# Three float32r layers on one core: starting addresses inside the SBUF arena shifted by 64 and 192 bytes

## The chip, the core and the metric

The kernel runs on one core of one Trainium2 chip. The metric is the device time of one execution in microseconds (us); here the median of three executions.

## What is computed

The reference puts three layers behind each other for one sequence of 512 tokens with 1,024 features, in float32. Cut to what matters:

```python
def first_block(x, ...):                        # DEPTH = 2
    for i in range(DEPTH):
        mix = ssd_mixer(x, ...) if i % 2 == 0 else hgrn2_mixer(x, ...)
        h = layer_norm(ALPHA * x + mix, ...)
        a = relu(h @ w1[i])                     # 1024 -> 4096
        h = layer_norm(ALPHA * h + (a * a) @ w2[i], ...)
        x = h + sigmoid(h @ w_gate[i]) * (p[i] @ w_proj[i])
    return x

def second_block(x, mem, positions, ...):       # DEPTH_2 = 1
    x = mla_layer(x, mem, ...)                  # 12 heads of 96, 4 memory heads of 64
    return rmsnorm(x, final_norm_g)
```

`ssd_mixer` is a state space layer in chunks of 128 tokens, `hgrn2_mixer` a gated linear recurrence with 8 heads. Nearly all of the arithmetic lies in the products with weights: the projections into and out of each mixer, the two MLPs, the gates.

## The kernel before

It is written by hand, engine by engine, with semaphores. Each engine has its own program in a block; the order on TensorE (PE) is fixed in the text.

**Split products.** A float32 product is made of three float32r products. Each operand is split into a high part (a float32r copy) and a low part (what the copy lost, rounded to float32r). For each 128-row slice k of the inner dimension, TensorE then multiplies high by high, high (stationary) by low (moving), low (stationary) by high (moving). `times_parts` (L889, the multiplication at L907) does so for the out-projections, both MLPs, the gates and most of the third layer; `passes` (L699, at L702) for the first layer's projections, the attention scores, the small projections of the third layer and the last product; an inner `passes` of `hgrn_project` (L1078, at L1081) for the HGRN heads, where the moving operand is 512 columns wide for two of the units and 256 for the other two; `gate_tile` (L988, at L1001) for the first tile of a gate. In a profile's name such as `psum<-w_lo,hid_hi` the moving operand stands first and the stationary one second. The stationary operand is 128 columns, and is loaded by a LDWEIGHTS of its own for every multiplication (PEld).

```python
for n_pass, (a, m_) in enumerate(((still_hi, moving_hi), (still_hi, moving_lo), (still_lo, moving_hi))):
    m = pe.matmul(psum[:, bank[c], cols or slice(0, width)], a, m_, start=..., stop=...)
```

**Where operands come from.** Weights come by DMA in units of 1,024 x 512 floats into two slots in turn (SP's queue). ScalarE (ACT) copies each unit to `w_hi` (L1654), VectorE (DVE) subtracts to `w_lo` (L2432), both slice by slice, behind TensorE's use of the previous unit. Activations are turned on TensorE, and their parts written by ACT (`f_hi`, `hid_hi`) and DVE (`f_lo`, `hid_lo`).

**The memory.** All buffers have fixed addresses in a partition of SBUF. `slots`, `res`, `rn`, `fT`, `gb` and `pT` are tensors of their own, each a multiple of 4,096 bytes long. After them lies the arena (L158) of 29,920 floats, which the stages share: `carve` (L169) hands out float32 views one after the other, `part` (L223) puts a float32r tensor at a given word of it, `over` (L226) one over the other tensors. The main ones, by word of the arena:

```python
yT_lo = [part("yT_lo_a", 13824, KD, T), part("yT_lo_b", 9728, KD, T)]
rings = [part(f"ring{n}", ring_first + n * KD * 256, KD, 256) for n in range(3)]   # ring_first = 17920
f_hi, f_lo = part("f_hi", 5632, KD, T), part("f_lo", 13824, KD, T)
w_hi, w_lo = part("w_hi", 17920, KD, HALF), part("w_lo", 22016, KD, HALF)
hid_hi, hid_lo = part("hid_hi", 0, KD, T), part("hid_lo", 9728, KD, T)
```

The arena begins at byte 103,328, which is 160 beyond a multiple of 256. So does every one of the tensors above, and so do the slots and `fT`: at L907 the moving operand and every stationary tile start at the same place within 256 bytes. A stationary tile is 512 bytes of a partition, a moving operand of 512 columns 2,048.

Of the kernel before, what the change touches and what calls it, by code (L numbers as in the profile page):

```python
# [12 lines left out]
F32R = mybir.dt.float32r  # L13
# [3 lines left out]
P = 128  # L17
T = 512
NT = T // P
D = 1024  # L20
KD = D // P
# [5 lines left out]
RMS_EPS = 1e-5  # L27
EPS = 1e-6
ARENA = 29920
DFF = 4 * D  # L30
KF = DFF // P
PLE = 256
# [18 lines left out]
NMEM = 256  # L51
MT = NMEM // P
# [45 lines left out]
    return c  # L98

class Banks:

# [28 lines left out]
def build(nc, x, p, cst, par_a, par_b, w_ssd, w_dt, dt_bias, a_log, d_skip, w_ssd_out, w_hgrn, w_hgrn_out,  # L132
          ln_g, ln_b, w_mlp1, w_mlp2, w_gate, w_proj, mem, pos, w_mla, w_uq, w_ukv, w_mem, w_mla_out, fin_g, out):
    with ExitStack() as ctx:
        def sb(name, shape, dt=F32):
            return ctx.enter_context(nc.sbuf_tensor(name, shape, dt))
# [18 lines left out]
        gb_base = nc.sbuf_base - 4 * 2 * D  # L155
        pT = sb("pT", [P, DEPTH, KP, T])
        pT_base = nc.sbuf_base - 4 * DEPTH * KP * T
        arena = sb("arena", [P, ARENA])  # L158
        arena_base = nc.sbuf_base - 4 * ARENA
        con = sb("con", [P, C_ALL])  # L160
        col_b = sb("col_b", [P, B_ROWS])
        eps_h = sb("eps_h", [P, 1])
# [4 lines left out]
        at = [0]  # L167

        def carve(*shape):  # L169
            n = int(np.prod(shape))  # L170
            assert at[0] + n <= ARENA, (at[0], n)
            v = arena[:, at[0]:at[0] + n]
            at[0] += n
            if len(shape) == 2:
                v = v.rearrange("p (a b) -> p a b", a=shape[0])
            if len(shape) == 3:
                v = v.rearrange("p (a b c) -> p a b c", a=shape[0], b=shape[1])
            return v

        xdt = carve(NT, HALF)
        xw = carve(NT, HALF)
        xr = carve(NT, HALF)
        zs = carve(NT, HALF)
        prev = carve(NT - 1, HALF)
# [27 lines left out]
        xdt_first, xw_first = 0, 2048  # L213
        dtT = zs[:, 0, :]
        s_par = prev[:, 0, 0:2 * P].rearrange("p (a n) -> p a n", a=2)
        s_p = [arena[:, 26112 + i * NT * PLE:26112 + (i + 1) * NT * PLE].rearrange("p (t n) -> p t n", t=NT)
               for i in range(DEPTH)]
        Mh = rn[:].rearrange("p t d -> p (t d)").rearrange("p (j l) -> p j l", j=S_HPG)
        bc_w = gb[:].rearrange("p a b -> p (a b)").rearrange("p (k n) -> p k n", k=KD)
# [1 line left out]

        def part(name, first, *shape):  # L223
            return nc.alloc_sbuf_tensor_at(name, [P, *shape], F32R, offset=arena_base + 4 * first)

        def over(name, base, *shape):  # L226
            return nc.alloc_sbuf_tensor_at(name, [P, *shape], F32R, offset=base)
# [2 lines left out]
        bc_lo = over("bc_lo", gb_base, KD, 256)  # L230
        x_lo, z_lo = over("x_lo", slots_base, KD, HALF), over("z_lo", slots_base + 4 * 4096, KD, HALF)
        rings = [part(f"ring{n}", ring_first + n * KD * 256, KD, 256) for n in range(3)]
        z_his = [part(f"z_hi{n}", ring_first + n * KD * 256, KD, HALF) for n in range(2)]
        yT_hi = [over("yT_hi_a", fT_base, KD, T), part("yT_hi_b", 0, KD, T)]
        yT_lo = [part("yT_lo_a", 13824, KD, T), part("yT_lo_b", 9728, KD, T)]
        sums_parts, picks = over("sums_parts", pT_base, T), over("picks", pT_base + 4 * T, S_HEADS)
# [14 lines left out]
        w_hi, w_lo = part("w_hi", 17920, KD, HALF), part("w_lo", 22016, KD, HALF)  # L251
        hid_hi, hid_lo = part("hid_hi", 0, KD, T), part("hid_lo", 9728, KD, T)

        sq = arena[:, 4096:4096 + 3 * T].rearrange("p (a l) -> p a l", a=3)
        sg = arena[:, 9728:9728 + 4096].rearrange("p (t d) -> p t d", t=NT)

        def pp(i, t):

            return pT[:, i, :, :].rearrange("p k l -> p (k l)") if t == NT - 1 else arena[:, 26112 + t * D:26112 + (t + 1) * D]

        first_hi, first_lo = over("first_hi", fT_base, KD, HALF), z_lo

# [60 lines left out]
        ukv_hi, ukv_lo = part("ukv_hi", 17920, KKV, A_HEADS * 2 * NOPE), part("ukv_lo", 22016, KKV, A_HEADS * 2 * NOPE)  # L323
        out_his = [part("out_hi0", 22016, KD, HALF), part("out_hi1", 16384, KD, HALF)]
        branch_lo = part("branch_lo", 0, KD, T)
        mem_tok = arena[:, 0:MT * D].rearrange("p (a b) -> p a b", a=MT)
        memT = arena[:, MT * D:MT * D + KD * NMEM].rearrange("p (a b) -> p a b", a=KD)
        gate = rn

# [1115 lines left out]
        def _(act):  # L1446
# [235 lines left out]
            def projected(stage, i, j):  # L1682

                t, h = j // NHALF, j % NHALF
                b = full(stage, (h, t))
                act.copy(pp(i, t)[:, h * HALF:(h + 1) * HALF], psum[:, b, :]).then_inc(bank_free[b], 1)
# [470 lines left out]
        def _(dve):  # L2157
# [405 lines left out]
            def half_gate(i, h, t):  # L2563

                cols = slice(h * HALF, (h + 1) * HALF)
                wait_taken(dve, f"gate{i}", (h, t))
                dve.wait_ge(res_ready, NT * (2 * i + 1) + t + 1)
                dve.tensor_tensor(sg[:, t, cols], sg[:, t, cols], pp(i, t)[:, cols], ALU.mult)
                dve.drain()
                dve.tensor_tensor(res[:, t, cols], res[:, t, cols], sg[:, t, cols], ALU.add)\  # L2570
                    .then_inc(sig(f"{('ple_first', 'ple_second')[h]}{i}"), 1)
# [585 lines left out]
```

## Time and profile before

| | |
|---|---|
| median of three executions | 1888.76 us (1887.98 to 1889.18) |
| the profiled execution | 1887.8 us, its span 1885.9 us |
| TensorE, multiplications | 1860.2 us (99%), 9,678 of them |
| TensorE, loads of the stationary operand | 1572.5 us (83%) |
| VectorE | 1139.6 us (60%) |
| ScalarE | 922.0 us (49%) |
| GpSimd | 178.1 us (9%) |
| granted TensorE clock | 0.998 of full speed |
| DMA | 162.02 MB, 86 GB/s over the span |

The time of the profiled execution is what the device reports; the span runs from its first to its last instruction, 1.9 us less. Busy time of PE counts each multiplication from its start to its modelled end; consecutive ones overlap, so the distance from one start to the next (the pace) says more than the 389 ns that one is listed with.

### The profile page before, as it was taken

The page shows a single profiled execution, that of the slowest core. Times are in us where ns is not written, and L with a number is a line of the kernel's source. Part 1 is how long each engine was busy: PE and PEld are TensorE (multiplying, and loading weights), DVE is VectorE, ACT ScalarE, POOL GpSimd, SP SyncE. Part 2 cuts the span into 40 slices and gives each one's busy share as a digit, 9 for nine tenths or more (in the row PEclk, how much of TensorE's full clock was granted, in tenths as well). Part 3 has the DMA queues.
Part 4 walks back from the last instruction along what each step waited for, and adds up shares of the span by engine and source line. Part 5 has one row for each costly group of instructions (what it writes and reads, how often), then busy time and mean ns, then how long its engine had stood idle before and what let it go on. Part 6 is the DMA issues. An engine that isn't in the chain of part 4 may idle for free.

```text
span 1885.9 us, 26981 instructions
## 1 busy us (share of the span) xinstructions
PE 1860.2 (99%) x9678; PEld 1572.5 (83%) x9678; DVE 1139.6 (60%) x2013; ACT 922.0 (49%) x1827; POOL 178.1 (9%) x137
## 2 busy tenths in 40 slices
PE   8999999999999999999999999999999999999998
PEld 7788787877888888899999977888888889887987
DVE  5677677557443434557887876634444587556765
ACT  5765765453332324546768655323333364535551
POOL 0201202004000000400101003100000220001100
PEclk9999999999999999999999999999999999999999
DMA  6131214314233222313312124323222222320001
GB/s 200 45 108 41 76 45 157 112 68 156 89 108 115 90 89 90 89 46 90 91 45 67 46 81 143 112 90 115 106 89 89 90 101 93 117 101 1 1 0 45
DMA packets 116738, 162.02 MB, mean 86 GB/s; under 512 B 6085, under 2 KB 57251, under 8 KB 116643
## 3 DMA queue, kind: packets, MB, share of 16 engines
q1 hardware_dynamic: 115347, 156.04, 24.8%
q0 software_dynamic: 1296, 4.72, 0.7%
q8 instruction: 59, 0.97, 0.2%
q14 instruction: 36, 0.29, 0.0%
HBM read 158.64 MB, written 2.10 MB: 85 GB/s over the span
## 4 chain that ended last, share of the span: by engine, by line
PE 92%; DVE 4%; ACT 3%; DVEq 1%; issue 0%; ACTq 0%; DMA 0%; SPq 0%
PE psum L907 52%; PE psum L702 15%; PE psum L1081 8%; PE psum L667 4%; PE psum L1114 3%; PE psum L1344 2%; PE psum L853 1%; PE psum L940 1%; DVE arena L2275 1%; DVE z_lo L2199 1%; PE psum L1001 1%; PE psum L860 1%; PE psum L848 1%; ACT rn L1548 1%; ACT arena L1542 0%; PE psum L1188 0%
## 5 line engine op out<-in xcount | busy, mean ns | idle before, releaser
L2432 DVE TENSOR_TENSOR w_lo<-slot,w_hi 128x512 fp32r<-128x512 f32 x304 | 232.9, 785 | 352.7 <-ACT w_hi L1654 352.6
L1654 ACT CAST w_hi<-slot 128x512 fp32r<-128x512 f32 x304 | 185.4, 623 | 426.0 <-PE psum L907 410.5
L907 PE MATMUL psum<-f_lo,w_hi 128*128 128x512 f32 x528 | 205.4, 389 | 0.0
L907 PE MATMUL psum<-f_hi,w_hi 128*128 128x512 f32 x512 | 199.8, 390 | 1.4 <-DVE f_lo L2480 1.0
L907 PE MATMUL psum<-w_hi,hid_hi 128*128 128x512 f32 x512 | 199.5, 390 | 0.0
L907 PE MATMUL psum<-w_hi,hid_lo 128*128 128x512 f32 x512 | 199.2, 389 | 0.0
L907 PE MATMUL psum<-w_lo,hid_hi 128*128 128x512 f32 x512 | 199.2, 389 | 0.0
L907 PE MATMUL psum<-f_hi,w_lo 128*128 128x512 f32 x512 | 199.2, 389 | 0.0
L3056 POOL TENSOR_TENSOR res<-rn,gb 128x1024 f32<-128x1024 f32 x16 | 46.2, 2888 | 838.5 <-DVE rn L2420 632.5
L907 PEld LDWEIGHTS psum<-f_lo,w_hi 128*128 128x128 f32 x528 | 99.1, 188 | 20.5 <-issue 0.2
L907 PEld LDWEIGHTS psum<-f_hi,w_hi 128*128 128x128 f32 x512 | 96.1, 188 | 22.9 <-DVE f_lo L2480 1.8
L907 PEld LDWEIGHTS psum<-w_hi,hid_lo 128*128 128x128 f32 x512 | 96.1, 188 | 20.1
L907 PEld LDWEIGHTS psum<-f_hi,w_lo 128*128 128x128 f32 x512 | 96.1, 188 | 20.1
L907 PEld LDWEIGHTS psum<-w_hi,hid_hi 128*128 128x128 f32 x512 | 96.1, 188 | 19.8
L907 PEld LDWEIGHTS psum<-w_lo,hid_hi 128*128 128x128 f32 x512 | 96.1, 188 | 19.7
L907 PE MATMUL psum<-w_hi,f_lo 128*128 128x512 f32 (+2 forms) x224 | 82.5, 368 | 0.0
L702 PE MATMUL psum<-in_hi,ring 128*128 128x512 f32 x192 | 77.0, 401 | 0.0
L702 PE MATMUL psum<-in_lo,ring 128*128 128x512 f32 x192 | 74.8, 389 | 0.0
L667 PE MATMUL psum<-con,arena 128*128 128x128 f32 (+1 forms) x486 | 70.4, 273 | 0.7 <-DVE branch_lo L2977 0.3
L2275 DVE SCALAR_TENSOR_TENSOR arena<-psum,col_a,arena 128x511 f32<-128x511 f32 (+2 forms) x72 | 53.4, 747 | 27.6 <-ACT arena L1536 24.0
L1081 PE MATMUL psum<-w_hi,f_hi 128*128 128x256 f32 x224 | 65.6, 293 | 0.0
L667 PEld LDWEIGHTS psum<-con,arena 128*128 128x128 f32 (+1 forms) x486 | 57.7, 146 | 7.5 <-issue 2.1
(388 smaller groups left out, 4376.1 us busy)
## 6 DMA issues: line engine op xcount, KB each, us to landing
slot<-in_w_mlp SPq DMA_DIRECT2D x128, 512.0 KB, 5.7
slot<-in_w_ssd SPq DMA_DIRECT2D x32, 512.0 KB, 5.8
slot<-in_w_hgrn SPq DMA_DIRECT2D x32, 512.0 KB, 6.7
slot<-in_w_ssd_out SPq DMA_DIRECT2D x16, 512.0 KB, 6.0
slot<-in_w_gate SPq DMA_DIRECT2D x16, 512.0 KB, 5.4
gb<-in_w_ssd SPq DMA_DIRECT2D x8, 512.0 KB, 7.9
slot<-in_w_hgrn_out SPq DMA_DIRECT2D x8, 512.0 KB, 5.8
slot<-in_w_mla SPq DMA_DIRECT2D x8, 512.0 KB, 5.3
```

Source lines behind the costliest of these rows:

```text
L667: return pe.transpose(psum[0:mp, b, cols:cols + kp], src, con[0:kp, C_ID:C_ID + kp])
L702: m = pe.matmul(out, a, m_, start=first and n_pass == 0, stop=last and n_pass == 2)
L848: pe.matmul(psum[:, b, :], Btok[:, c, :], xw[:, c, :], start=True, stop=True).then_inc(bank_full[b], 1)
L853: m = pe.matmul(psum[:, b, j * S_P:(j + 1) * S_P], Mh[:, j, c * P:(c + 1) * P], xdt[:, c, j * S_P:(j + 1) * S_P], start=True, stop=True)
L907: m = pe.matmul(psum[:, bank[c], cols or slice(0, width)], a, m_, start=opens and k == 0 and n_pass == 0, stop=closes and k == KD - 1 and ...
L1081: m = pe.matmul(out, a, m_, start=k == 0 and n_pass == 0, stop=k == KD - 1 and n_pass == 2)
L1114: m = pe.matmul(psum[:, b, c * P:(c + 1) * P], a, a, start=True, stop=True)
L1344: m = pe.matmul(psum[:, b, (t - 1) * V_HEAD:t * V_HEAD], probT[:, (t - 1) % 2, c * P:(c + 1) * P], values(c), **first_and_last(c, nk))
L1654: act.copy(w_hi[:, k, :], as_k(slot_of(stage, n))[:, k, :]).then_inc(high_made, 1)
L2275: m = dve.scalar_tensor_tensor(cv[:, n % 3, back:T], psum[:, b, 0:T - back], col_a[:, at_:at_ + 1], cv[:, n % 3, back:T], ALU.mult, ALU.add)
L2432: dve.tensor_tensor(w_lo[:, k, :], as_k(slot_of(stage, n))[:, k, :], w_hi[:, k, :].bitcast(F32), ALU.subtract).then_inc(low_made, 1)
L3056: pool.tensor_tensor(res[:, t, :], rn[:, t, :], gb[:, 0, :], ALU.mult).then_inc(sig("res_scaled"), 1)
```

## The change

```diff
+GUARDS = ((5632, 0), (9728, 16), (13824, 16), (17920, 16), (22016, 48), (26112, 48))
+ARENA_WORDS = ARENA + GUARDS[-1][1]
...
+def placed(word):
+    return word + max([guard for first, guard in GUARDS if first <= word], default=0)
...
-        arena = sb("arena", [P, ARENA])
-        arena_base = nc.sbuf_base - 4 * ARENA
+        arena = sb("arena", [P, ARENA_WORDS])
+        arena_base = nc.sbuf_base - 4 * ARENA_WORDS
...
-            v = arena[:, at[0]:at[0] + n]
+            v = arena[:, placed(at[0]):placed(at[0]) + n]
...
         def part(name, first, *shape):
-            return nc.alloc_sbuf_tensor_at(name, [P, *shape], F32R, offset=arena_base + 4 * first)
+            at_, n = placed(first), int(np.prod(shape))
+            whole = nc.alloc_sbuf_tensor_at(name, [P, at_ % 8 + n], F32R, offset=arena_base + 4 * (at_ - at_ % 8))
+            v = whole[:, at_ % 8:at_ % 8 + n]
+            return v.rearrange("p (a b) -> p a b", a=shape[0]) if len(shape) == 2 else v
...
-        sq = arena[:, 4096:4096 + 3 * T].rearrange("p (a l) -> p a l", a=3)
-        sg = arena[:, 9728:9728 + 4096].rearrange("p (t d) -> p t d", t=NT)
+        sq = arena[:, placed(4096):placed(4096) + 3 * T].rearrange("p (a l) -> p a l", a=3)
+        sg = arena[:, placed(9728):placed(9728) + 4096].rearrange("p (t d) -> p t d", t=NT)
```

Starts within 256 bytes, counted from the old common one:

| buffers | before | changed |
|---|---|---|
| `hid_hi`, `f_hi`, `yT_hi_b`, `o_hi`, `branch_lo`; outside the arena `in_hi`, `in_lo`, `x_lo`, `z_lo`, `bc_lo`, `m_hi`, `yT_hi_a`, slots | 0 | 0 |
| `hid_lo`, `f_lo`, `yT_lo`, `o_lo` | 0 | 64 |
| `w_hi`, `ring0`, `ring1`, `z_hi`, `qT_hi`, `kT_hi`, `kT_lo`, `out_hi1`, `ukv_hi` | 0 | 64 |
| `w_lo`, `ring2`, `out_hi0`, `ukv_lo` | 0 | 192 |
| `con` (the identity that transposes are made with) | 128 | 64 |

## Rows read from the trace of the kernel before

**Rows 1.** the page, part 1, busy time of each engine, and TensorE's clock in part 2.
```profile
PE 1860.2 (99%) x9678; PEld 1572.5 (83%) x9678; DVE 1139.6 (60%) x2013; ACT 922.0 (49%) x1827; POOL 178.1 (9%) x137
...
PEclk9999999999999999999999999999999999999999
```

**Rows 2.** waits of PE: who ended them, us in total, times, longest.
```profile
PE psum L667 <- DMA rn<-in_x: 5.0, 1, 5.0
PE psum L780 <- ACT rn L1548: 3.6, 4, 1.1
```

**Rows 3.** stretches: all of L907, then L1081, L1001 and L702, on PE and PEld.
```profile
0.00:1886.00 1886.00, 985.32 (x4368) 811.72 (x4368) 1.00 0.26 86
0.00:1886.00 1886.00, 165.52 (x1008) 144.85 (x1008) 1.00 0.26 86
0.00:1886.00 1886.00, 22.61 (x96) 17.88 (x96) 1.00 0.26 86
0.00:1886.00 1886.00, 383.60 (x1692) 297.66 (x1692) 1.00 0.26 86
```

**Rows 4.** timeline of PE in the first MLP: first and last of 28 rows.
```profile
589.24 0.39 PE L907 MATMUL psum<-w_hi,hid_hi 128*128 128x512 f32 x1
...
595.36 0.39 PE L907 MATMUL psum<-w_hi,hid_hi 128*128 128x512 f32 x1
```

**Rows 5.** timeline of PE: 13 rows of L1081, then 18 of L907 at 288 columns.
```profile
879.74 0.28 PE L1081 MATMUL psum<-w_lo,f_hi 128*128 128x256 f32 x1
...
881.18 0.28 PE L1081 MATMUL psum<-w_lo,f_hi 128*128 128x256 f32 x1
1592.87 0.29 PE L907 MATMUL psum<-w_hi,m_hi 128*128 128x288 f32 x1
...
1593.40 0.29 PE L907 MATMUL psum<-w_lo,m_hi 128*128 128x288 f32 x1
1593.52 0.29 PE L907 MATMUL psum<-w_hi,f_lo 128*128 128x288 f32 x1
...
1595.10 0.29 PE L907 MATMUL psum<-w_hi,f_lo 128*128 128x288 f32 x1
```

**Rows 6.** timeline of PE after a pause, 13 rows of L702 in all.
```profile
141.30 0.39 PE L702 MATMUL psum<-z_hi,in_hi 128*128 128x512 f32 x1
...
142.00 0.39 PE L702 MATMUL psum<-z_hi,in_hi 128*128 128x512 f32 x1
142.22 0.39 PE L702 MATMUL psum<-z_lo,in_hi 128*128 128x512 f32 x1
...
143.38 0.39 PE L702 MATMUL psum<-z_hi,in_hi 128*128 128x512 f32 x1
...
144.06 0.39 PE L702 MATMUL psum<-z_hi,in_hi 128*128 128x512 f32 x1
```

**Rows 7.** timeline of PE: sixteen transposes, then plain float32 multiplications, 256 columns.
```profile
1558.89 1.91 PE L667 MATMUL psum<-con,rn 128*128 128x128 f32 x16
1562.58 5.13 PE L1239 MATMUL psum<-arena,slot 128*128 128x256 f32 x23
```

**Rows 8.** timeline, PE and PEld: a multiplication and the load that follows it.
```profile
141.53 0.40 PE L702 MATMUL psum<-z_lo,in_hi 128*128 128x512 f32 x1
141.53 0.19 PEld L702 LDWEIGHTS psum<-z_hi,in_lo 128*128 128x128 f32 x1
```

**Rows 9.** stretches: part of the first MLP, then of HGRN, all engines.
```profile
440.00:778.00 338.00, 338.00 (x1501) 280.06 (x1500) 155.78 (x241) 112.88 (x198) 15.13 (x8) 1.00 0.29 103
900.00:1000.00 100.00, 99.86 (x718) 93.57 (x717) 80.36 (x143) 72.97 (x147) 9.08 (x8) 1.00 0.26 66
```

**Rows 10.** the page, part 5: DVE and ACT splitting weights.
```profile
L2432 DVE TENSOR_TENSOR w_lo<-slot,w_hi 128x512 fp32r<-128x512 f32 x304 | 232.9, 785 | 352.7 <-ACT w_hi L1654 352.6
L1654 ACT CAST w_hi<-slot 128x512 fp32r<-128x512 f32 x304 | 185.4, 623 | 426.0 <-PE psum L907 410.5
```

More of the change, by code:

```diff
@@ L215, in build @@
         s_par = prev[:, 0, 0:2 * P].rearrange("p (a n) -> p a n", a=2)
-        s_p = [arena[:, 26112 + i * NT * PLE:26112 + (i + 1) * NT * PLE].rearrange("p (t n) -> p t n", t=NT)
+        s_p = [arena[:, placed(26112) + i * NT * PLE:placed(26112) + (i + 1) * NT * PLE].rearrange("p (t n) -> p t n", t=NT)
                for i in range(DEPTH)]
@@ L252, in build @@
         hid_hi, hid_lo = part("hid_hi", 0, KD, T), part("hid_lo", 9728, KD, T)
-        sq = arena[:, 4096:4096 + 3 * T].rearrange("p (a l) -> p a l", a=3)
-        sg = arena[:, 9728:9728 + 4096].rearrange("p (t d) -> p t d", t=NT)
+        sq = arena[:, placed(4096):placed(4096) + 3 * T].rearrange("p (a l) -> p a l", a=3)
+        sg = arena[:, placed(9728):placed(9728) + 4096].rearrange("p (t d) -> p t d", t=NT)
         def pp(i, t):
-            return pT[:, i, :, :].rearrange("p k l -> p (k l)") if t == NT - 1 else arena[:, 26112 + t * D:26112 + (t + 1) * D]
+            return pT[:, i, :, :].rearrange("p k l -> p (k l)") if t == NT - 1 else arena[:, placed(26112) + t * D:placed(26112) + (t + 1) * D]
         first_hi, first_lo = over("first_hi", fT_base, KD, HALF), z_lo
@@ L325, in build @@
         branch_lo = part("branch_lo", 0, KD, T)
-        mem_tok = arena[:, 0:MT * D].rearrange("p (a b) -> p a b", a=MT)
-        memT = arena[:, MT * D:MT * D + KD * NMEM].rearrange("p (a b) -> p a b", a=KD)
+        mem_tok = arena[:, placed(0):placed(0) + MT * D].rearrange("p (a b) -> p a b", a=MT)
+        memT = arena[:, placed(MT * D):placed(MT * D) + KD * NMEM].rearrange("p (a b) -> p a b", a=KD)
         gate = rn
```

## The prediction

> **What bounds the kernel now.** I read the page first. TensorE is busy 1860.2 of 1885.9 us, so it idles 26 us in all, and its clock stands at full speed in every slice, which is the 2.4 GHz level [rows 1]. The waits of PE then show that no other engine holds it up for long: the longest is 5.0 us for the first rows of x, the next group 3.6 us in four pieces [rows 2]. In the first MLP PE is never idle, DVE works 156 of 338 us and ACT 113; in the HGRN stage, the tightest, DVE works 80 and ACT 73 of 100 us while PE works 99.9 [rows 9]. So only a different pace on TensorE moves the end, and a pace of TensorE moves it nearly one to one.
>
> The pace is therefore the thing to read. In the MLP 27 starts of 512 columns take 595.36 - 589.24 = 6.12 us, 226.7 ns each [rows 4]. At 2.4 GHz 512 columns are 213.3 ns, so each multiplication costs 13.3 ns more than its columns. At 256 columns it is 1.44 us / 12 = 120.0 ns against 106.7, again 13.3 more; at 288 columns 2.23 us / 17 = 131.2 against 120.0, only 11.2 more [rows 5]. There the starts are not even: most are 130 to 140 ns apart, but one is 120 (1593.40 to 1593.52, to 10 ns). The mean fits three at 133.3 and one at 126.7, as if a multiplication paid either two or one piece of 6.67 ns, the time of 16 columns, which is 64 bytes.
>
> Plain float32 multiplications read 256 columns at half that rate, and need (5.13 - 0.38) / 22 = 215.9 ns against 213.3 [rows 7] (0.38 is the length of the last one): they pay 2.6 ns, not 13.3. So some 10.7 ns of each float32r multiplication are not a fixed price of an instruction. And after a pause the extra is not constant: nine starts take 2.08 us, 231.1 ns each, among them one of 240 and one of 220 (to 10 ns), until the stream falls into 226.7 (142.00, 142.22, then 143.38 to 144.06 for three) [rows 6]. Something that depends on how two things lie against each other in time costs TensorE between 7 and 27 ns per multiplication. The stationary tile of the next multiplication begins to load in the same 10 ns in which the present one begins to stream [rows 8], and in the old placement both begin at the same place within 256 bytes. The natural suspect is that both reads go to the same part of SBUF at the same time.
>
> **The change part by part.** No instruction is added or moved, so the sum has one term: what the pace becomes where the two reads now start apart.
>
> How many: for every multiplication of float32r I set the moving operand's start against the start of the next stationary tile. They differ now at 4,352 of the 4,368 of L907, 987 of the 1,008 of L1081, 64 of the 96 of L1001, 932 of the 1,692 of L702 [rows 3] and 9 of L780's: 6,344. The other third of L702 keeps distance 0, since `in_lo` and `x_lo` or `z_lo` both stay where they were, and so do most of the small projections. The distances are 64 bytes one way or the other where high meets high, and 128 where low meets low. How a multiplication's operands lie against its own tile does not count in this picture, since that tile is loaded before.
>
> What each saves, bounded by the nearest rows: at most 13.3 - 2.6 = 10.7 ns, the float32 price [rows 7], which is 6,344 x 10.7 ns = 68 us. At least nothing. And it can lose: the stream after a pause averages 231.1, 4.4 ns more, 28 us in all, and its worst starts are near 236, 9 ns more, 59 us. I take the middle step, one piece of 6.67 ns, since that is the one smaller price that a steady stream pays here (one start in four at 288 columns [rows 5]), and since both streams still run through the same memory at different speeds: the moving one covers 512 bytes in 53 ns, while the load of 512 bytes is listed with 0.19 us [rows 8], so one overtakes the other whatever the distance at the start. That is 6,344 x 6.67 ns = 42.3 us.
>
> How much of it reaches the end: DVE and ACT keep the same work. In the MLP they have room for far more than the 3% by which TensorE would speed up. In HGRN the chain of DVE is 80% full [rows 9]; what TensorE gains there may partly come back as waits, which I put at 1 us in all, an estimate. The loads take 0.29 of the DMA engines' time there. Splitting weights costs DVE 785 ns and ACT 623 ns for a slice [rows 10]; DVE now reads the slot at distance 0 and `w_hi` at 64 and writes `w_lo` at 192, which could make it quicker or slower, and either is covered: DVE waits 352.7 us before these slices and ACT 426.0. Transposes use `con`, which moves from 128 to 64 bytes away from `rn`: they go at (1.91 - 0.27) / 15 = 109 ns [rows 7], 2.6 ns over the 106.7 that 128 columns take at half rate, so they had no piece to lose, and I cost them at nothing.
>
> Sum: 1887.8 - 42.3 + 1 = 1846.5 us for the profiled execution. The median stands 1 us above that execution, so 1847 us.
>
> **The rivals.**
> *Both pieces go* (0.23). If the overlap at the start causes everything, the extra falls to the float32 price: 1888.8 - 68 = 1821 us. For it: the old placement is the one in which everything begins together. Against it: the overtaking above.
> *Nothing changes* (0.21): the extra is a price of reading four bytes per column at full rate while any load runs, wherever the two lie. Thirteen ns are 32 columns, and a stationary tile of 512 bytes is 32 pieces of 16 bytes: one column lost per piece would give just this, at 256 columns as at 512. Then 1888.8 us. For it: 13.3 at both widths [rows 4, 5], and the transposes that already had distance 128 show nothing. Against it: one start in four at 288 columns, and the uneven starts after a pause.
> The Trainium skill says the same from the other side: SBUF — State Buffer, "Who interferes with whom", gives TensorE two independent read ports and ends with "PE and ACT never wait on anyone". By that rule an address cannot matter, and the change would be worth nothing. The trace does not show such independence: the extra of 7 to 27 ns is there [rows 6]; but nothing in it shows an address either.
> *The lock is lost* (0.20, slower): at distance 0 every multiplication has the same partner, and the stream settles at 226.7 after about nine starts. Now the distance alternates, 64, 128, 64, so the state in which the two reads lie well may never be reached, and the stream stays as it is after a pause: 231.1 instead of 226.7, 28 us, 1917 us. It decides from an average extra above 13.3 ns on. For it: that the settled state is a better one than those around it [rows 6]. Against it: the loss needs the average of the new distances to be worse than distance 0, where the streams start on top of each other.
> The remaining 0.02 are small losses elsewhere, a DVE slowed by its three operands in HGRN among them.
> That the change does not do what it says is excluded by the addresses: the tensors do start where the table puts them.
>
> **How the numbers follow.** The forecast, a gain of one piece, has 0.34, with its own range from 1835 to 1865 us for a mix of pairs that lose one, two or none. Gains hold 0.34 + 0.23 = 0.57, no change (within 0.2%, 3.8 us, about what a measurement of this kernel can tell) 0.21, losses 0.22. The range leaves out most of the losing side and a little below the full gain: from 1816 to 1893 us.
>
> **What would show it.** In the profile after: starts in the MLP 220 ns apart, so 455 multiplications of L907 per 100 us where there were 443; if both pieces go, 216 ns; if nothing, 226.7; if the lock is lost, starts of changing distance with a mean near 231. Products of L702 in the first layer should then be mixed: their middle multiplication, whose reads keep distance 0, should stay slower than its neighbours if the address at the start matters. The float32 rows and the transposes should not move. The prediction is wrong if the pace at L907 is unchanged or longer, and wrong in its reasoning, even at the right time, if L702's middle ones gain as much as the others, or if the gain comes from a wait of TensorE.

## The result, and the profile after

| | before | changed |
|---|---|---|
| median | 1888.37 us (1887.92 to 1889.18, 4 executions) | 1907.3 us (1906.89 to 1907.43, 4 executions) |
| ratio | | 1.0101, 95% interval 1.0088 to 1.0114 |
| the profiled execution, span | 1885.9 us | 1904.9 us |
| forecast | | 1847 us, 1816 to 1893 |

The changed kernel is 18.9 us slower. The forecast had the sign wrong, and its range ends 14 us too low. Ratios, here and below, compare executions in the fast state alone (of the ten executions of `e_256` further down, one took 3798.27 us and is not in its ratio). In the changed kernel every line from the table on lies 11 further down (L907 is L918, L1081 L1092, L702 L713, L667 L678, L1239 L1250).

The page of the changed kernel, parts 1, 2 and 5:

```profile
PE 1880.2 (99%) x9678; PEld 1569.5 (82%) x9678; DVE 1139.7 (60%) x2013; ACT 921.2 (48%) x1827; POOL 178.5 (9%) x137
...
PEclk9999999999999999999999999999999999999999
...
L2443 DVE TENSOR_TENSOR w_lo<-slot,w_hi 128x512 fp32r<-128x512 f32 x304 | 233.5, 786 | 363.8 <-ACT w_hi L1665 363.7
L1665 ACT CAST w_hi<-slot 128x512 fp32r<-128x512 f32 x304 | 184.7, 620 | 438.9 <-PE psum L918 422.9
```

The waits of PE, changed kernel (us in total, times, longest):

```profile
PE psum L678 <- DMA rn<-in_x: 5.5, 1, 5.5
PE psum L791 <- ACT rn L1559: 2.5, 4, 1.0
```

TensorE is busy 20.0 us longer at the same count and the same clock ([rows 1]: 1860.2). It still idles 25 us in all, and its two longest groups of waits moved by 0.5 and -1.1 us [rows 2]. DVE and ACT split a slice in the same time as before, 786 and 620 ns (785 and 623), and wait 11 and 13 us longer for it, ACT for TensorE, which is later, and DVE for ACT [rows 10]. So the whole difference is TensorE's own pace.

Stretches over the whole span, changed kernel: L918, L1092, L1012, L713 (PE busy, PEld busy, clock, DMA):

```profile
0.00:1908.00 1908.00, 1001.34 (x4368) 811.26 (x4368) 1.00 0.26 85
0.00:1908.00 1908.00, 164.84 (x1008) 142.97 (x1008) 1.00 0.26 85
0.00:1908.00 1908.00, 22.94 (x96) 17.88 (x96) 1.00 0.26 85
0.00:1908.00 1908.00, 388.19 (x1692) 297.35 (x1692) 1.00 0.26 85
```

Against [rows 3] L918 has 16.0 us more, L713 4.6, L1012 0.3, and L1092 0.7 less. The four make 20.3 us, which is the whole of it.

Timeline of PE in the changed kernel: the first MLP, where activations move ("up"), then where weights move ("down"), at two places; then HGRN; then sixteen transposes and plain float32 multiplications. A row has start, length, engine, line, and out<-moving,stationary:

```profile
455.12 0.39 PE L918 MATMUL psum<-f_hi,w_hi 128*128 128x512 f32 x1
...
461.36 0.40 PE L918 MATMUL psum<-f_hi,w_hi 128*128 128x512 f32 x1
...
499.98 0.39 PE L918 MATMUL psum<-w_hi,hid_hi 128*128 128x512 f32 x1
...
506.16 0.39 PE L918 MATMUL psum<-w_hi,hid_hi 128*128 128x512 f32 x1
...
589.91 0.40 PE L918 MATMUL psum<-w_hi,hid_hi 128*128 128x512 f32 x1
...
596.15 0.39 PE L918 MATMUL psum<-w_hi,hid_hi 128*128 128x512 f32 x1
...
889.12 0.28 PE L1092 MATMUL psum<-w_hi,f_lo 128*128 128x256 f32 x1
...
890.53 0.28 PE L1092 MATMUL psum<-w_hi,f_lo 128*128 128x256 f32 x1
...
1576.08 1.91 PE L678 MATMUL psum<-con,rn 128*128 128x128 f32 x16
1577.82 7.07 PE L1250 MATMUL psum<-arena,slot 128*128 128x256 f32 x32
```

In the up half 27 starts now take 6.24 us, 231.1 ns each, where they took 6.12 and 226.7 [rows 4]: 17.8 ns over the 213.3 of the columns instead of 13.3. In the down half they take 6.24 us at 589.91, but 6.18 us, 228.9 ns each, at 499.98: 17.8 and 15.6 ns over the columns, with the same buffers at the same addresses. More on that below. At 256 columns 12 starts take 1.41 us, 117.5 ns: 10.8 over the columns instead of 13.3 [rows 5], so there the change does bring something. Transposes take 1.91 us for sixteen as before, and plain float32 (7.07 - 0.38) / 31 = 215.8 ns from record to record [rows 7]. (The code has 16 plain float32 multiplications at L1250 and the trace 32 records: each multiplication leaves two of them.)

Added up over all records of float32r multiplications, from start to start less the columns at 2.4 GHz (gaps of over 50 ns left out), the extra is:

| columns | before | changed |
|---|---|---|
| 512 | 81.6 us | 104.2 us |
| 256 | 11.0 us | 8.7 us |
| 384 and 288 | 3.9 us | 3.8 us |
| all | 96.5 us | 116.7 us |

That is 20.2 us more, against 19.0 by which the span grew: 22.6 lost at 512 columns and 2.3 won at 256.

The clearest rows are at the very end of the kernel. In the last product `out_hi` is the only operand that moved; `x_lo`, `m_hi` and the next tile `branch_lo` lie where they lay. Timeline of PE, changed kernel, 19 rows of L713:

```profile
1884.78 0.39 PE L713 MATMUL psum<-out_hi,branch_lo 128*128 128x512 f32 x1
...
1885.24 0.39 PE L713 MATMUL psum<-x_lo,m_hi 128*128 128x512 f32 x1
1885.47 0.40 PE L713 MATMUL psum<-out_hi,branch_lo 128*128 128x512 f32 x1
...
1885.93 0.40 PE L713 MATMUL psum<-x_lo,m_hi 128*128 128x512 f32 x1
1886.17 0.39 PE L713 MATMUL psum<-out_hi,branch_lo 128*128 128x512 f32 x1
...
1888.97 0.39 PE L713 MATMUL psum<-out_hi,branch_lo 128*128 128x512 f32 x1
```

The 18 starts take 4.19 us, 232.8 ns each. The multiplication with the moving `x_lo`, whose own distances are all 0, takes 0.23 or 0.24 us like its neighbours, where the same stream stood at 226.7 before. A multiplication pays for its neighbours' addresses too.

### The profile page after: what moved, and what is told of

It is laid out like the page before. It is cut to its first block, busy times and chain, and to the rows that moved or that the text cites. A ratio compares the mean times of both kernels' runs of the same rounds, so it can differ in the third digit from the quotient of the medians.

```text
span 1904.9 us, 26981 instructions
## 1 busy us (share of the span) xinstructions
PE 1880.2 (99%) x9678; PEld 1569.5 (82%) x9678; DVE 1139.7 (60%) x2013; ACT 921.2 (48%) x1827; POOL 178.5 (9%) x137
## 4 chain that ended last, share of the span: by engine, by line
PE 92%; DVE 4%; ACT 3%; DVEq 1%; issue 0%; ACTq 0%; DMA 0%; SPq 0%
PE psum L918 52%; PE psum L713 15%; PE psum L1092 8%; PE psum L678 4%; PE psum L1125 3%; PE psum L1355 2%; PE psum L864 1%; PE psum L951 1%; DVE arena L2286 1%; DVE z_lo L2210 1%; PE psum L1012 1%; PE psum L871 1%; PE psum L859 1%; ACT rn L1559 1%; ACT arena L1553 0%; PE psum L1199 0%
## 5 line engine op out<-in xcount | busy, mean ns | idle before, releaser
L918 PE MATMUL psum<-f_lo,w_hi 128*128 128x512 f32 x528 | 206.2, 390 | 0.0
L918 PE MATMUL psum<-f_hi,w_hi 128*128 128x512 f32 x512 | 203.3, 397 | 1.4 <-DVE f_lo L2491 1.0
L918 PE MATMUL psum<-w_hi,hid_hi 128*128 128x512 f32 x512 | 201.5, 394 | 0.0
L918 PE MATMUL psum<-f_hi,w_lo 128*128 128x512 f32 x512 | 201.2, 393 | 0.0
L918 PE MATMUL psum<-w_lo,hid_hi 128*128 128x512 f32 x512 | 200.9, 392 | 0.0
L918 PE MATMUL psum<-w_hi,hid_lo 128*128 128x512 f32 x512 | 199.6, 390 | 0.0
L918 PEld LDWEIGHTS psum<-f_lo,w_hi 128*128 128x128 f32 x528 | 99.2, 188 | 22.5 <-issue 0.2
L918 PEld LDWEIGHTS psum<-f_hi,w_hi 128*128 128x128 f32 x512 | 96.2, 188 | 23.9 <-DVE f_lo L2491 1.8
L918 PEld LDWEIGHTS psum<-f_hi,w_lo 128*128 128x128 f32 x512 | 96.0, 188 | 23.7
L918 PEld LDWEIGHTS psum<-w_hi,hid_lo 128*128 128x128 f32 x512 | 96.1, 188 | 21.9
L918 PEld LDWEIGHTS psum<-w_hi,hid_hi 128*128 128x128 f32 x512 | 95.9, 187 | 22.1
L918 PEld LDWEIGHTS psum<-w_lo,hid_hi 128*128 128x128 f32 x512 | 96.1, 188 | 20.9
L918 PE MATMUL psum<-w_hi,f_lo 128*128 128x512 f32 (+2 forms) x224 | 82.5, 368 | 0.0
L713 PE MATMUL psum<-in_hi,ring 128*128 128x512 f32 x192 | 77.4, 403 | 0.0
L713 PE MATMUL psum<-in_lo,ring 128*128 128x512 f32 x192 | 75.8, 395 | 0.0
L678 PE MATMUL psum<-con,arena 128*128 128x128 f32 (+1 forms) x486 | 70.4, 274 | 0.4 <-DVE branch_lo L2988 0.4
L1092 PE MATMUL psum<-w_hi,f_hi 128*128 128x256 f32 x224 | 64.9, 290 | 0.0
L678 PEld LDWEIGHTS psum<-con,arena 128*128 128x128 f32 (+1 forms) x486 | 57.8, 146 | 7.2 <-issue 1.7
```

The source lines that it names most:

```text
L678: return pe.transpose(psum[0:mp, b, cols:cols + kp], src, con[0:kp, C_ID:C_ID + kp])
L713: m = pe.matmul(out, a, m_, start=first and n_pass == 0, stop=last and n_pass == 2)
L1092: m = pe.matmul(out, a, m_, start=k == 0 and n_pass == 0, stop=k == KD - 1 and n_pass == 2)
```

## The experiments

Two theories stood at the start. **Place:** something about where the operands lie in absolute terms. **Distance:** how moving and stationary operand lie to each other within some period; with three readings, that the alternation 64, 128, 64 is what costs (the rival of the prediction), that each multiplication has a price by its own distance, or that the cycle of three has one.

### Where the buffers lie, and whether the distance alternates

`e_shift` is the kernel before with one tensor of 64 bytes ahead of everything; `e_unif` the changed kernel with another table:

```diff
+        pad = sb("pad", [P, 16])
```

> The kernel before with a pad of 64 bytes in front of all buffers: every address moves, no distance between two buffers does. Theory (distances between TensorE's two reads): no change, 1888 to 1889 us, 226.7 ns per start in the MLP. Rival (absolute place): a change of up to 1% either way, as in the changed kernel.

```diff
-GUARDS = ((5632, 0), (9728, 16), (13824, 16), (17920, 16), (22016, 48), (26112, 48))
+GUARDS = ((5632, 0), (9728, 0), (13824, 0), (17920, 16), (22016, 16), (26112, 16))
```

> The changed kernel with another table: both parts of the weights and all behind them start 64 bytes further on, both parts of the activations stay. The distance is 64 bytes in all passes (one way in the products with moving activations, the other way where weights move). Theory that the alternation of distances costs the time: the stream locks again, 1885 to 1892 us. Rival that distance 64 is itself worse than 0: slower by as much as the changed kernel, near 1907 us.

Measured: `e_shift` 1888.49 us, ratio to before 0.9999 (0.9989 to 1.0008). A common shift of 64 bytes changes nothing, so place is out as far as this tests it. `e_unif`, in which nothing alternates within the up half or within the down half, 1910.55 us, 1.0115 (1.0098 to 1.0132), as slow as the changed kernel or slower; 1885 to 1892 us had been expected if the alternation were to blame. So the alternation is not needed; a constant distance of 64 bytes costs as much.

### The price of each distance

`m1` measures the price by itself: no layers, TensorE alone, 39 multiplications per distance, each stretch behind one of 64 columns. This and the three measurements like it (`m2`, `m3`, `m4`) were executed once each.

```diff
+            for c, (width, mh, ml, sh, sl) in enumerate(cases()):
...
+                    moving = (5632 + mh, 13824 + ml, 5632 + mh)[n_pass] + 512 * k
+                    still = (17920 + sh, 17920 + sh, 22016 + sl)[n_pass] + 512 * k
+                    pe.matmul(psum[:, c % 6, 0:width], buf[:, still:still + P], buf[:, moving:moving + width],
+                              start=n_pass == 0, stop=n_pass == 2)
```

> Not the kernel but a measurement: nothing is computed of the reference, x is written out as it came. TensorE alone runs stretches of 39 float32r multiplications in the kernel's order of the three passes; no other engine reads or writes meanwhile. In each stretch the moving operand starts a fixed number of bytes beyond the place where the stationary tiles start (0 to 496 bytes in steps of 16, then 512 to 2048 in steps of 256 at 512 columns; 0 to 480 in steps of 32 at 256 columns). Theory (two reads of TensorE meet in SBUF): distance 0 gives 226.7 ns per start again, other distances give other paces between about 216 and 236 ns, and the pattern repeats after 256 or 512 bytes. Rival (the other engines' traffic or the absolute address causes the change): every stretch has the same pace, 226.7 ns at 512 columns and 120 at 256.

Timeline of PE in `m1`; a row is one stretch. The moving operand lies ahead by 16, 64, 128, 192, 256 and 272 bytes; then 256 columns, 0 and 32 bytes:

```profile
58.32 9.28 PE L58 MATMUL psum<-buf 128*128 128x512 f32 x39
...
85.88 9.19 PE L58 MATMUL psum<-buf 128*128 128x512 f32 x39
...
122.39 9.30 PE L58 MATMUL psum<-buf 128*128 128x512 f32 x39
...
159.22 9.34 PE L58 MATMUL psum<-buf 128*128 128x512 f32 x39
...
196.10 9.10 PE L58 MATMUL psum<-buf 128*128 128x512 f32 x39
205.07 9.28 PE L58 MATMUL psum<-buf 128*128 128x512 f32 x39
...
405.69 4.92 PE L58 MATMUL psum<-buf 128*128 128x256 f32 x39
410.48 4.80 PE L58 MATMUL psum<-buf 128*128 128x256 f32 x39
```

A row holds the restless first multiplications too, so its mean, (9.34 - 0.39) / 38 = 235.5 ns, lies some 2 ns above the settled pace. The mean of the last 18 distances between starts, less the columns, is the price (ns):

| moving ahead by, bytes | 0 | 16 | 32, 48 | 64 | 80 | 96 | 112 | 128 | 144 | 160 | 176, 192 | 208 | 224, 240 | 256 |
|---|---|---|---|---|---|---|---|---|---|---|---|---|---|---|
| 512 columns | 13.3 | 18.2 | 20.0 | 15.6 | 17.8 | 20.0 | 17.8 | 18.7 | 20.0 | 21.1 | 20.0 | 21.3 | 20.0 | 13.3 |

From 256 on it repeats (272: 18.2), and 512 to 2,048 in steps of 256 all give 13.3. At 512 columns 0 is the best distance, not the worst. At 256 columns 0 and 96 are the worst, with 13.3, and 32 bytes the best with 10.0; that is the gain of the HGRN rows. The granted clock was 1.0, and no other engine worked meanwhile, so the extra needs neither DVE nor ACT nor DMA. That is what the theory of the expectation said, but for one thing: it allowed paces down to 216 ns, and none at 512 columns is below 226.7.

`m2` runs all 64 combinations of where low activations, high weights and low weights start, 36 multiplications each:

```diff
+    return [(512, 0, ml, sh, sl) for sh in (0, 16, 32, 48) for sl in (0, 16, 32, 48) for ml in (0, 16, 32, 48)]
```

> A measurement like the one before, with 64 stretches of 36 multiplications at 512 columns: the high moving operand stays where it is, the low moving one and the high and low tiles each start 0, 64, 128 or 192 bytes further on, all combinations. Theory that the settled state is lost when the distance changes from pass to pass: the stretches in which all three passes have the same distance settle at one pace, those in which it changes do not and average 229 to 232 ns; the two combinations that the changed kernel has in its MLP (low moving 64, high tile 64, low tile 192; and low moving 128, high tile 192, low tile 0) give 230 to 231. Rival that only the distance of each pass counts, each on its own: the mean of a mixed stretch is the mean of the paces that its three distances have in uniform stretches.

Timeline of PE in `m2`: the table of the change with activations moving (low 64, high weights 64, low weights 192), then with weights moving (128, 192 and 0, counted from the high part that moves), then the best that has any shift (64, 192, 64):

```profile
295.21 8.57 PE L51 MATMUL psum<-buf 128*128 128x512 f32 x36
...
472.62 8.57 PE L51 MATMUL psum<-buf 128*128 128x512 f32 x36
...
498.05 8.45 PE L51 MATMUL psum<-buf 128*128 128x512 f32 x36
```

Settled: 17.7, 17.8 and 14.5 ns; all other shifted ones lie between 15.5 and 22.2, and only all at 0 comes to 13.3. So the change's 17.8 is found with TensorE alone. The mean of the single prices would be (20.0 + 18.7 + 20.0) / 3 = 19.6 for the first, so the rival that each distance has its price, alone, is out: a cycle of three has its own price. Nor do all stretches with one distance to the next tile settle at one pace, as was expected: three stretches in which every next tile lies at distance 0, but not every own tile, cost 17.8, 17.7 and 20.0.

### The table, tried on the kernel

Three more tables, each in both kinds of units; for `e_256` and `e_mild` the arena is 16 words shorter.

```diff
-GUARDS = ((5632, 0), (9728, 16), (13824, 16), (17920, 16), (22016, 48), (26112, 48))
+GUARDS = ((5632, 0), (9728, 64), (13824, 64), (17920, 64), (22016, 64), (26112, 64))
```

> The changed kernel with another table: everything from word 9728 of the arena on starts 256 bytes further on (the arena's unused last 16 words are given up for it). Theory (only the distance within 256 bytes counts, which the first measurement showed to repeat every 256): all distances are as before, so 1886 to 1891 us and 226.7 ns per start in the MLP. Rival (the buffers of the old placement were good for another reason, such as their place within 2,048 bytes): slower by 0.3% or more.

```diff
-GUARDS = ((5632, 0), (9728, 16), (13824, 16), (17920, 16), (22016, 48), (26112, 48))
+GUARDS = ((5632, 0), (9728, 32), (13824, 32), (17920, 32), (22016, 64), (26112, 64))
```

> The changed kernel with another table: low activations and high weights start 128 bytes further on, low weights 256. Theory A (the pace is a property of the whole cycle of three passes, as measured in the 64 stretches): 15.5 ns over the columns for both kinds of product, 228.8 ns per start in the MLP, 2.2 ns x 4,368 = 9.6 us at L907 and some more at L702: 1895 to 1904 us, so quicker than the changed kernel with its smaller shifts. Theory B (each pass pays the price of its own distance, alone): distance 128 bytes in every pass, 18.7 ns, 232.0 per start, 5.4 x 4,368 = 23 us: 1908 to 1918 us.

```diff
-GUARDS = ((5632, 0), (9728, 16), (13824, 16), (17920, 16), (22016, 48), (26112, 48))
+GUARDS = ((5632, 0), (9728, 16), (13824, 16), (17920, 16), (22016, 32), (26112, 32))
```

> The changed kernel with another table: low activations and high weights start 64 bytes further on, low weights 128. Theory A (the cycle of three passes): 19.9 and 20.0 ns over the columns in the two kinds of product, 233.3 ns per start in the MLP, 6.7 x 4,368 = 29 us and some more at L702: 1914 to 1926 us. Theory B (each pass by its own distance): 20.0 where weights are the tiles, 15.6 where they move, 17.8 in the mean, 4.4 x 4,368 = 19 us: 1904 to 1912 us.

| kernel | price of the cycle by `m2`, up / down | in the kernel, up / down | extra summed, against before | span against before | median, ratio (95%) |
|---|---|---|---|---|---|
| `e_256` | 13.3 / 13.3 | as before | +0.2 us | +0.8 us | 1889.20, 1.0002 (0.9992 to 1.0012) |
| `e_mild` | 15.5 / 15.5 | 15.7 / 15.7 | +11.8 us | +11.9 us | 1899.90, 1.0054 (1.0037 to 1.0071) |
| the change | 17.7 / 17.8 | 17.8 / 16.7 | +20.2 us | +19.0 us | 1907.30, 1.0101 (1.0088 to 1.0114) |
| `e_unif` | 20.0 / 15.6 | 20.0 / 16.6 | +23.1 us | +23.7 us | 1910.55, 1.0115 (1.0098 to 1.0132) |
| `e_hard` | 19.9 / 20.0 | 20.0 / 19.9 | +31.7 us | +30.3 us | 1917.09, 1.0144 (1.0127 to 1.0161) |

"Up" is `f_hi`, `f_lo` moving, "down" `hid_hi`, `hid_lo` stationary; prices are ns over the columns, and "in the kernel" is the mean over the three kinds of start, all stretches together. The stretches of L918 over the whole span say the same in busy time (PE, PEld, clock, DMA). In `e_256`:

```profile
0.00:1920.00 1920.00, 985.67 (x4368) 811.92 (x4368) 1.00 0.25 84
```

The same stretch of L918 in `e_mild`:

```profile
0.00:1920.00 1920.00, 994.43 (x4368) 811.14 (x4368) 1.00 0.25 84
```

And in `e_hard`:

```profile
0.00:1920.00 1920.00, 1010.72 (x4368) 811.59 (x4368) 1.00 0.25 84
```

With 985.32 before [rows 3] and 1001.34 in the changed kernel they stand in the order of the table. All three medians lie in the ranges that theory A, or the theory of the distance within 256 bytes, had given, and outside those of their rivals. A shift by 256 bytes costs nothing, so only the place within 256 bytes counts. In `e_mild` every distance to the next tile is 128 bytes, whose single price in `m1` is 18.7; the cycle's price is 15.5, and the kernel pays 15.7. In `e_hard` the down half has only distances of 64 (single price 15.6), the cycle's price is 20.0, and the kernel pays 19.9. So the cycle of three has the price, not the single multiplication.

Two entries do not fit: "down" is 16.7 where `m2` gave 17.8 (the change), and 16.6 where it gave 15.6 (`e_unif`). Both are means of two different steady paces. Timeline of PE in `e_unif`, down, 27 starts each at two places:

```profile
500.03 0.39 PE L918 MATMUL psum<-w_hi,hid_lo 128*128 128x512 f32 x1
...
506.21 0.39 PE L918 MATMUL psum<-w_hi,hid_lo 128*128 128x512 f32 x1
...
589.87 0.40 PE L918 MATMUL psum<-w_hi,hid_lo 128*128 128x512 f32 x1
...
596.17 0.40 PE L918 MATMUL psum<-w_hi,hid_lo 128*128 128x512 f32 x1
```

That is 6.18 us and 6.30 us, 228.9 and 233.3 ns each, 15.6 and 20.0 over the columns. The kernel has eight long down stretches, of 48 or 64 cycles of three multiplications. In the changed kernel four settle at 15.6 and four at 17.8, in turn; in `e_unif` six at 15.6 and two at 20.0; in `before` all eight at 13.3. Each keeps its pace to the end, and all eight use the same buffers. So the addresses do not fix the pace alone: away from the common start a stream can have more than one steady state. The last multiplication of the up half took 229 ns before each stretch at 15.6 in the changed kernel and 235 or 236 before each one at 17.8; in `e_unif` it took 233 before the two at 20.0 and 229 or 236 before the others. This points to the moment at which a stretch is entered, but no run varied it alone.

### What the extra is made of

`m3` holds one of the two reads on a single word, and tries other strides, distances and widths:

```diff
+    if step == 0:
+        return buf[:, first:first + 1].broadcast_to([P, n])
+    return buf[:, first:first + n * step:step]
```

> A measurement like the first two, stretches of 30 float32r multiplications: tiles read with a step of 0, 1, 2 and 4 words, the moving operand with a step of 0 (one word read over and over), distances of 1 to 7 words, widths of 64 to 480 columns at distance 0, and three stretches in plain float32. Theory (the extra over the columns comes from the two reads meeting in the same part of SBUF): with the tile's read held on one word or the moving one held on one word the extra changes clearly, and with both held it is largest or vanishes; plain float32 stays at 2 to 3 ns over 426.7 at every distance. Rival (13.3 ns are a fixed price of float32r that other distances only add to): no stretch is below 13.3 ns at 512 columns, the held ones included.

Timeline of PE in `m3`: the distance of 192 bytes; the tile held on one word; the tile read at a stride of 16 bytes (distance 192); the moving operand held on one word (distance 0); the same with the tile held as well:

```profile
70.33 7.24 PE L76 MATMUL psum<-buf 128*128 128x512 f32 x30
77.44 7.19 PE L76 MATMUL psum<-buf 128*128 128x512 f32 x30
...
156.09 7.50 PE L76 MATMUL psum<-buf 128*128 128x512 f32 x30
163.46 6.72 PE L76 MATMUL psum<-buf 128*128 128x512 f32 x30
...
189.80 6.72 PE L76 MATMUL psum<-buf 128*128 128x512 f32 x30
```

Settled: 20.0, 17.8, 24.9, 2.5 and 2.5 ns. With the moving operand held, the extra is 2.5 at every distance tried, the price of plain float32 [rows 7]. So 10.8 of the old 13.3 ns come from the moving operand's walk through memory, and how much it costs depends on the tile's addresses: 13.3 to 26.7 ns over all cases here (26.7 for a distance of 20 bytes, and for a tile of stride 16 bytes at 64 and 128). Holding the tile on one word does not remove it. What a multiplication would cost without any load beside it was not tried, so it stays open how much belongs to the meeting of the two reads and how much to the moving one alone. Plain float32 leaves two records per multiplication, 429 ns each for 512 columns at distances 0, 64 and 128, 2.5 over the 426.7 of half rate. The rival of the expectation, 13.3 as a fixed price, is out. At distance 0 the widths 320, 384 and 512 pay 13.3 and 288, 352, 416, 448 and 480 pay 11.6, 14.4, 15.2, 16.0 and 16.7.

### Next tile, own tile, or the whole sequence

The prediction counted only the distance to the next tile. In the last measurement both operands drift by s bytes from one multiplication to the next, and the tile starts o bytes further on than its own moving operand, so the next tile starts s + o bytes further on (all within 256 bytes):

```diff
+                    k = 576 * (i % 8)
+                    moving = 5632 + k + (step * i) % 64
+                    still = 17920 + k + (step * i + off) % 64
```

> A measurement, not the layers: x is copied to the output, TensorE alone works, the computation of the reference is left out. Stretches of 39 multiplications. In every multiplication the moving operand starts s bytes further within 256 bytes than in the one before, and its own stationary tile starts o bytes behind it, so that the next tile starts s + o bytes behind it; s and o each 0, 64, 128 or 192. The prices with s = 0 are to repeat the first table: o = 0 gives 13.3 ns over the columns, o = 64 (the moving one lies 192 ahead) 20.0, o = 128 18.7, o = 192 (64 ahead) 15.6. Theory N, only the next tile counts (the picture of the prediction): the extra depends on s + o alone; s = 192, o = 64 gives 13.3 although it never lies on its own tile, and s = 64, o = 0 gives 20.0 although it always does. Theory O, only the own tile counts: the extra depends on o alone; s = 64, o = 0 gives 13.3 and s = 192, o = 64 gives 20.0. Theory S, the whole sequence of addresses counts, since what one read is delayed by shifts the next: neither holds, and only s = 0, o = 0 comes to 13.3. The same at 256 columns with o = 0 and 128. Last, s = 0 with a first multiplication of 96, 160, 224 or 288 columns in place of 64: if the settled pace depends on how a stream began, the four differ by over 0.5 ns; if on the addresses alone, they agree.

Timeline of PE in `m4`, s and o: 0 and 64; 64 and 0; 192 and 64:

```profile
58.04 9.35 PE L54 MATMUL psum<-buf 128*128 128x512 f32 x39
...
85.47 9.23 PE L54 MATMUL psum<-buf 128*128 128x512 f32 x39
...
167.43 9.33 PE L54 MATMUL psum<-buf 128*128 128x512 f32 x39
```

| settled extra, ns (last 24 distances) | o = 0 | 64 | 128 | 192 |
|---|---|---|---|---|
| s = 0 | 13.3 (13.8 in the first stretch) | 20.0 | 18.8 | 15.5 |
| s = 64 | 17.2 | 15.0 | 18.8 | 18.3 |
| s = 128 | 15.0 | 16.7 | 16.7 | 20.0 |
| s = 192 | 18.3 | 19.8 | 18.3 | 18.3 |

Neither of the simple theories holds. Where the next tile has distance 0 (64 and 192, 128 and 128, 192 and 64) it costs 18.3, 16.7 and 19.8; where the own tile has, 17.2, 15.0 and 18.3. Only with everything at one place is it 13.3. With s = 0 and a first multiplication of 96, 160, 224 or 288 columns the settled extra is the same within 0.1 ns at o = 0, 64 and 192, and 18.8 to 19.3 at 128, where the pattern is longer than what was averaged. So the whole sequence of addresses counts. How the stream began made no difference in this measurement; in the kernel, equal addresses did settle in two ways (the down stretches above), so what four lengths of a first multiplication did not bring about is not excluded.

No version here beats the kernel before. At 512 columns nothing came below 13.3 but the held operand, which computes something else. At 256 columns a distance of 32 bytes would save 3.3 ns on the 672 such multiplications of HGRN, 2.2 us, an estimate, hardly more than the interval of a ratio here (0.1%, 1.9 us).

## Why the prediction was wrong

**What bounds the kernel** was right. A change of TensorE's pace went to the end one to one: 20.2 us summed from starts, 19.0 in the span. That the old 13.3 ns are no fixed price, and that the part above 2.6 ns depends on how two reads lie to each other, was right too: `m3` gets to 2.5, `m1` shows 13.3 to 21.3 by distance alone.

**The step that failed** is "I take the middle step, one piece of 6.67 ns": the price of a distance other than 0 was put at -6.67 ns and is +4.4 ns in the up halves of the MLPs (13.3 to 17.8) and +3.3 in the down halves (13.4 to 16.7). Behind it stood the sentence that in the old placement "both begin at the same place within 256 bytes. The natural suspect is that both reads go to the same part of SBUF at the same time". No row showed that a common start is bad; the runs show that at 512 columns it is the best placement of all that were tried. The rows showed the reverse: with the same addresses, the stream before it settled paid 231.1 [rows 6], so other states of the same two reads were dearer than the settled one. The one smaller price was read at 288 columns; `m3` gives 11.6 ns there on average, at distance 0, with nothing moved, so it belongs to the width and says nothing of an address. Three readings were coarse besides. The start "120" away is 127 ns away in the trace, whose times the rows round to 10 ns. For the same reason "between 7 and 27 ns" after the pause is 11 to 23 (starts of 224 to 236 ns). And 215.9 ns is a record of plain float32, of which a multiplication has two; the 2.6 ns are per record.

**The bound** "at most 13.3 - 2.6 = 10.7 ns" took a price that comes without the walk of the moving operand at full rate for one that an address could give. No address gave less than 13.3 at 512 columns.

**The count** of 6,344 multiplications rested on the picture that "how a multiplication's operands lie against its own tile does not count". It does (`m4`), and so do the neighbours': the third of L702 that was to keep its price lost as well, `z_lo,in_hi` from 14.0 to 21.1 ns and `x_lo,m_hi` from 13.7 to 22.5, means over 128 and 32 starts. The prediction had named these as the ones that would stay as they were.

**The rivals.** *Both pieces go* and *Nothing changes* fell with the result. *The lock is lost* had the sign, the pace of the up halves (231.1, the very number, by luck: it was read from another stream after a pause) and 1917 us against 1907.3; most of the 10 us is what was won at 256 columns and what did not change at 384, which it had priced like 512, and the rest the down stretches at 228.9. Its mechanism is half right. The settled state at distance 0 is the good one, as it said; but other distances also settle into repeating patterns, only dearer ones (229, 228, 228 in `m4`; 230, 233, 241, 232, 231, 232, 228 in `m1`), at some placements into more than one, and the alternation is not needed (`e_unif`). It deserved more than 0.20: its only counter-argument was the same unshown assumption as the forecast's.

**The Trainium skill's rule**, SBUF — State Buffer, "Who interferes with whom", that PE never waits on anyone, had been read as leaving the time unchanged. As far as it speaks of other engines the runs agree: with all of them idle `m1` pays the 13.3 ns of the kernel before. The two independent read ports that the same section gives PE are not borne out for float32r: 13.3 to 26.7 ns per multiplication by the two operands' addresses and strides. The Trainium skill's TensorE: Matmul & The Clock Gate says in "Step-by-step: what each phase is for" that the next tile's load takes no read bandwidth from the running multiplication; what `m3` shows is a running multiplication whose pace changes when only the tiles' stride does (13.3 to 23.3 ns from 4 to 16 bytes, at distance 0).

**HGRN.** The 1 us of waits was meant for a TensorE that gains a piece there, and was not put to the test: from the first to the last record of L1081 the stage went from 225.3 to 224.8 us, and the idle time of PE in it from 0.2 to 0.4 us. Splitting weights, transposes and plain float32 cost what they had cost, as forecast.

## What to carry over

When float32r multiplications of 512 columns each come with their own tile load, start all their operands, moving and stationary, at the same place within 256 bytes; here each departure cost 1.2 to 9 ns of 227 per multiplication at multiples of 16 bytes. At the common start every long stretch also settled at the same 13.3 ns, which not every other placement gives. At 256 columns the advice does not hold (below). A shift of SBUF addresses is a change of TensorE's pace: look at starts in the steady stream and in the restless one behind a pause before assuming which way it goes. A stream that settles to a lower pace than it starts with has something to lose by a change of placement; a story about where reads collide needs a row that shows the collision.

## What the runs showed of the hardware that was not expected

The pace of a stream of float32r multiplications, each with its own tile load, depends on its operands' addresses within 256 bytes. A common shift of 64 bytes (`e_shift`) and the other engines (`m1`, `m2`) did not matter. At 512 columns it runs from 226.7 to 240.0 ns (distances of 0 and 20 bytes), and is 215.8 with the moving operand held on one word. With equal addresses it can settle at two paces: 228.9 or 231.1 ns in the down halves of the changed kernel, 228.9 or 233.3 in `e_unif`. The best distance depends on the width: 0 at 512 columns (13.3 ns over the columns), 32 bytes at 256 (10.0 against 13.3), and 0 or 64 bytes at 384 (13.3 both). At 64, 128 and 192 columns the mean distance between starts is 112 ns whatever the width (`m3`); that the tile loads set this pace is likely, but was not tested.
